# 96 token slots per expert in place of 128, operands 96 columns wide

## The chip, the cores and the metric

The kernel runs on one core of one Trainium2 chip. The metric is device time in microseconds (us). Before the change the median of three runs is 1418.41 us (1418.29 to 1418.92).

## The reference

Two decoder layers over 256 tokens of width 1024, all in fp32. Layer 0 is an mLSTM with memory attention and a dense SwiGLU. Layer 1 is multi-head latent attention with memory attention and an expert SwiGLU: the router picks 2 of 8 experts for each token. The part that matters here:

```
def moe_ffn(h, router, w_gate_up, w_down):        # D 1024, D_FF 3584, 8 experts, 256 tokens
    logits = t @ router
    top_v, top_i = lax.top_k(logits, 2)
    gates = softmax(top_v)
    for e in range(8):
        out = out + combine[:, e] * swiglu(t, w_gate_up[e], w_down[e])
```

512 assignments fall on 8 experts, 64 on the average expert. The weights of one expert are 44 MB, of all eight 352 MB.

## The kernel before, in words

Every fp32 product is made of three products of a rounded type (fp32r): each operand is cut into a high part (the value rounded) and a low part (the rest), and TensorE sums high x high, high x low and low x high in PSUM. ScalarE writes the high part of the weights (`expert_hi`, L799), VectorE the low part (`expert_lo`, L1884: ring minus high). SyncE streams weights into a ring of six slots of 1 MB (`load_expert`, L540), each slot filled by two transfers of 512 KB; it fills a slot again when its low part has been made (semaphore `lows`). High and low parts have three buffers (`CUTS`), which come free when TensorE is through with them (`through`).

The expert stage begins after the routing. Instead of all 256 tokens, an expert sees `CAP` slots: its tokens' rows are gathered into slots, 128 of them; an empty slot carries some row with gate 0, whose result goes to a spare row. If an expert has more than `CAP` tokens, all eight experts run again for the rest: `more` counts these further passes, and it is computed on the chip from the largest count. `PASSES` is 256/CAP rounded up; it bounds `more` and sets the size of the slot table in DRAM.

The order of the work is written out by hand, engine by engine; every engine walks the same loops. `expert(0)` stands alone, `Fori` runs the middle experts, and the last is again its own. An expert has seven blocks (`NBE`) of 512 hidden columns. A block is six cuts of 1 MB of weights: four for gate and up (`expert_gate_up`), two for down of the block before it (`expert_down`). A cut is 12 matmuls (`expert_cut`, L1718 to L1733): the activations are the stationary operand (128 rows of the contraction x `CAP` columns, one column for each slot), the weights are the moving operand, 512 columns wide. Then:

- ScalarE applies silu to the gate (L824, `silE`), VectorE multiplies by up (L1981, `hnE`): `CAP` partitions x 512.
- TensorE turns that with four transposes (`turn_expert`, through `tr`, L1162): source as stationary operand, identity as moving operand.
- ScalarE and VectorE cut the turned rows into high and low parts (`hidden_high` L804, `hidden_low` L1890), four chunks of `CAP` columns (`hhiE`, `hloE`).
- Next expert's rows: POOL fetches them with an indirect DMA, VectorE turns them in 32x32 squares (`turn_rows`, L1944, 16 instructions an expert, 4 in each of blocks 2 to 5), ScalarE and VectorE cut them (L759, L1960). The second expert's rows are turned by TensorE (eight transposes), the first expert's are gathered by matmuls with a matrix of zeros and ones, `Sx` (`gather`, L1689).
- An expert's result is scaled by the gate (`y_out`, L747) and added into DRAM by an indirect DMA.

The routing (`choose`, `put_slot`, L2439 to L2471) and `gates` (L1896 to L1910) are chains of small VectorE operations, each of which waits for the one before it. `gates` runs in block 2 of the first expert and computes each token's place in the slot table.

Of the kernel before, what the change touches and what calls it, by code (L numbers as in the profile page):

```python
# [18 lines left out]
ALU = mybir.AluOpType  # L19
# [4 lines left out]
I32 = mybir.dt.int32  # L24
U32 = mybir.dt.uint32

P = 128
# [1 line left out]
SLOTS = 6  # L29
SLOT = 2048  # L30
CUTS = 3
CAP = 128
NEG = -float(2.0 ** 100)
ROPE_THETA = 10000.0

# [1 line left out]
def build(nc, T, out):  # L37
    SEQ, D = T["x"].shape[1:]
    NT = SEQ // P
# [16 lines left out]
    NE = T["moe_router"].shape[2]  # L56
    HR = ROPE // 2
    assert NT == 2 and KD == 8 and NMEM == SEQ and MW == 256 and AH == 4 and BH == 6 and NOPE == P and VH == P
    PASSES = -(-SEQ // CAP)
    assert CAP <= P  # L60

    x_d, mem_d = T["x"][0], T["mem"][0]

# [91 lines left out]
    with ExitStack() as ctx:  # L155
# [5 lines left out]
        def S(name):  # L161
            if name not in sems:
                sems[name] = ctx.enter_context(nc.semaphore(name))
            return sems[name]
# [61 lines left out]
        def carve(at, *shape):  # L226
            n = int(np.prod(shape))
            v = arena[:, at:at + n]
            if len(shape) == 1:
# [36 lines left out]
        hn = carve(NT * FB, NT, FB)  # L266
        hT = carve(4096, 2, SEQ)
        silE, hnE = carve(0, EB)[0:CAP], carve(NT * FB, EB)[0:CAP]
        hhiE, hloE = (h[:, :, :].rearrange("p a s -> p (a s)")[:, 0:4 * CAP].rearrange("p (c s) -> p c s", s=CAP)
                      for h in (hhi, hlo))  # L270

        qF = carve(0, NT * BH, QKH)
# [17 lines left out]
        PT = carve(0, BH, 384)  # L290

        o = 2 * NT * FB
        Sx = carve(o, NT, CAP); o += NT * CAP
        tok_f = carve(o, NT); o += NT
        gate, gate_next = carve(o, 1)[0:CAP], carve(o + 1, 1)[0:CAP]; o += 2
        xe_ = slice(0, CAP)
        NC = PASSES * NE
        iota = carve(o, CAP); o += CAP
        iotai = arena[:, o:o + CAP].bitcast(I32); o += CAP
        m8 = carve(o, NT, 8); o += NT * 8  # L300
        idxf = carve(o, NT, 8); o += NT * 8
        idx8 = arena[:, o:o + NT * 8].bitcast(U32).rearrange("p (a b) -> p a b", a=NT); o += NT * 8
        oh1 = carve(o, NT, NE); o += NT * NE
        oh2 = carve(o, NT, NE); o += NT * NE
        picked = carve(o, NT + 1, NE); o += (NT + 1) * NE
        first_slot = carve(o, CAP); o += CAP
        key = carve(o, NT); o += NT
        ranks = carve(o, NT, NE); o += NT * NE
        hits = carve(o, 2, NT, NE); o += 2 * NT * NE
        place_at = carve(o, 3, 2 * NT); o += 6 * NT  # L310
        place_i = arena[:, o:o + 2 * NT].bitcast(I32); o += 2 * NT
        pay = carve(o, 2, NT, 3); o += 6 * NT
        raw = carve(o, 2, 3)[0:CAP]; o += 6
# [282 lines left out]
        def _(pool):  # L596
# [64 lines left out]
            for t in range(NT):  # L661
                pool.dma_start(xn[:, t], bass.AP(g1.tensor, g1.offset, [[0, P]] + [list(d) for d in g1.ap])).then_inc(S("g1_in"), 16)
            pool.wait_ge(S("att_out"), 1)
            pool.iota(iotai, pattern=[[1, CAP]], base=0, channel_multiplier=0).then_inc(S("iota"), 1)
            pool.wait_ge(S("iota"), 1)
            pool.tensor_copy(iota, iotai).then_inc(S("iota"), 1)
            pool.iota(tok_i, pattern=[[P, NT]], base=0, channel_multiplier=1).then_inc(S("iota"), 1)
# [2 lines left out]
            pool.wait_ge(S("iota"), 4)  # L670
            pool.tensor_scalar(first_slot, iota, 1.0, None, ALU.add).then_inc(S("iota"), 1)
            pool.memset(blank[:, :, 0], 0.0).then_inc(S("iota"), 1)
            pool.tensor_copy(blank[:, :, 1], iota[0:NC + 1]).then_inc(S("iota"), 1)
            pool.tensor_scalar(blank[:, :, 2], iota[0:NC + 1], float(SEQ), None, ALU.add).then_inc(S("iota"), 1)
            pool.wait_ge(S("iota"), 8)
            pool.dma_start(table_d.rearrange("(a s) c -> a s c", s=CAP), blank).then_inc(S("table_in"), 16)
            pool.dma_start(acc[SEQ:SEQ + CAP].rearrange("s (a n) -> s a n", n=P), over(ones[0:CAP, :], KD)).then_inc(S("table_in"), 16)
# [480 lines left out]
        def _(pe):  # L1158
# [527 lines left out]
            def gather(t, ks):  # L1686

                for k in ks:
                    last = mm(PS[:, 6 + k // KH, (k % KH) * CAP:(k % KH + 1) * CAP], lhsT=xn[:, t, k * P:(k + 1) * P], rhs=Sx[:, t, :],  # L1689
                              start=(t == 0 and k % KH == 0), stop=(t == NT - 1), skip_group_check=True)  # L1690
                return last

# [119 lines left out]
        def _(dve):  # L1812
# [80 lines left out]
            def gates():  # L1893

                dve.wait_ge(S("gate2_exp"), 1)
                then(v.tensor_scalar(gt2[:, 4:6], gt2[:, 2:4], 1.0, None, ALU.add))  # L1896
                then(v.reciprocal(gt2[:, 6:8], gt2[:, 4:6]))
                then(v.tensor_tensor(gt2[:, 8:10], gt2[:, 6:8], gt2[:, 2:4], ALU.mult))
                ends = [list(d) for d in ranks.ap]
                both = bass.AP(oh1.tensor, oh1.offset, ends[:1] + [[NT * NE, 2], [NE, NT], [1, NE]])  # L1900
                then(v.tensor_tensor(hits, both, bass.AP(ranks.tensor, ranks.offset, ends[:1] + [[0, 2], [NE, NT], [1, NE]]), ALU.mult))
                then(v.tensor_reduce(place_at[:, 0].rearrange("p (c t) -> p c t", c=2), hits, AX.X, ALU.add))
                then(v.tensor_scalar(place_at[:, 1], place_at[:, 0], float(CAP), float((NE - 1) * CAP), ALU.is_ge, ALU.mult))
                then(v.tensor_tensor(place_at[:, 2], place_at[:, 0], place_at[:, 1], ALU.add))
                then(v.scalar_tensor_tensor(out=place_at[:, 1].rearrange("p (c t) -> p c t", c=2), in0=bass.AP(idxf.tensor, idxf.offset, ends[:1] + [[1, 2], [NE, NT]]),
                                            scalar=float(CAP), in1=place_at[:, 2].rearrange("p (c t) -> p c t", c=2), op0=ALU.mult, op1=ALU.add))
                then(v.tensor_copy(place_i, place_at[:, 1]))
                v.tensor_copy(pay[:, :, :, 0], gt2[:, 6:10].rearrange("p (c t) -> p c t", c=2))
                for w in (1, 2):
                    last = v.tensor_copy(pay[:, :, :, w], over(tok_f, 2))  # L1910
                last.then_inc(S("gates"), 1)

            def next_dispatch(i, last):

                if isinstance(i, int):
                    dve.wait_ge(S("raw_in"), 32)
                    then(v.tensor_copy(gate, raw[:, 0, 0:1]))
                    then(v.tensor_copy(put_tok, raw[:, 0, 2:3]))
                    return
                dve.wait_ge(S("putting"), i)  # L1920
                dve.wait_ge(S("scattered"), i * 16)
                then(v.tensor_copy(gate, gate_next))
                then(v.tensor_copy(put_tok, put_next))
                if last:
                    for t in range(NT):
                        part = v.tensor_scalar(put_at[:, t:t + 1], put_next, float(t * P), None, ALU.subtract)
                    part.then_inc(S("dispatch"), 1)
                    dve.wait_ge(S("dispatch"), 3)
                    for t in range(NT):
                        part = v.tensor_scalar(Sx[:, t], iota, put_at[:, t:t + 1], None, ALU.is_equal)  # L1930
                    part.then_inc(S("dispatch"), 1)

            def next_slots(i):
# [6 lines left out]
            def turn_rows(squares):  # L1940

                for n in squares:
                    (r, c), last = divmod(n, 4), n == 15
                    done = v.transpose(xsT[32 * c:32 * c + 32].rearrange("p k (q s) -> p k q s", q=4)[:, :, r, :],  # L1944
                                       xs[32 * r:32 * r + 32].rearrange("p (k q f) -> p k q f", k=KD, q=4)[:, :, c, :])
                if last:
                    done.then_inc(S("gathered"), 1)
# [14 lines left out]
            def expert(i, last=False):  # L1962
                first = is_first(i)
                for b in range(NBE):
                    if b == 0 and not first:
                        expert_lo(i, 0, 0)
                        expert_lo(i, 0, 1)
                    if b > 0 or not first:
                        expert_lo(i, b, 2)
                        hidden_low(i * NBE + (NB + b))  # L1970
                    expert_lo(i, b, 3)
                    if b == 2 and not first and not last:
                        dve.wait_ge(S("fetching"), i)
                        next_slots(i)
                    if b > 0 or not first:
                        expert_lo(i, b, 4)
                        expert_lo(i, b, 5)
                    else:
                        expert_lo(i, 1, 0)
                    dve.wait_ge(S("silu"), i * NBE + (NB + b + 1))  # L1980
                    v.tensor_tensor(hnE, PS[0:CAP, expert_bank(i, b) + 1, :], silE, ALU.mult).then_inc(S("h_ready"), 1)  # L1981
                    if first and b == 2:
                        gates()
                    if b == (6 if first else 4 if last else 1):
                        next_dispatch(i, last)
                    if b == 5 and first:
                        next_slots(i)
                    if b < NBE - 1:
                        if b > 0 or not first:
                            expert_lo(i, b + 1, 0)  # L1990
                        expert_lo(i, b + 1, 1)
                    if 1 < b < 6 and not first and not last:
                        if b == 2:
                            dve.wait_ge(S("rows_in"), i * 16 + 16)
                        turn_rows(range(4 * (b - 2), 4 * (b - 1)))
                if not last:
                    gathered(i + 1, by_vector=not first)

# [448 lines left out]
            def put_slot(t):  # L2447

                then(v.scalar_tensor_tensor(out=key[:, t:t + 1], in0=rank_of[t][:, 0:1], scalar=1.0, in1=picked[:, t, 0:1], op0=ALU.add, op1=ALU.mult))
                return v.tensor_scalar(Sx[:, t], first_slot, key[:, t:t + 1], None, ALU.is_equal)  # L2450

            dve.wait_ge(S("iota"), 8)
            choose(0).then_inc(S("chosen"), 1)
# [66 lines left out]
```

## Time and profile before

| | |
|---|---|
| median of the runs | 1418.41 us |
| span of the profiled execution | 1417.7 us |
| TensorE matmuls busy | 1411.1 us (100%), 6721 instructions |
| weight loads busy | 1185.2 us (84%) |
| VectorE busy | 1234.8 us (87%) |
| ScalarE busy | 964.5 us (68%) |
| POOL busy | 101.9 us (7%) |
| read from HBM | 434.88 MB, 312 GB/s over the span |

Busy times of matmuls overlap: a matmul's record lasts longer than the distance to the next one's start. So a busy TensorE says little by itself, and the starts of its instructions say more. The profiled execution gives only its span; what a run's time has beyond it lies around the span.

### The profile page before, as it was taken

The numbers are of one execution on the slowest core, as the hardware profiler recorded it, in microseconds if no ns is written. First come the engines' busy times: TensorE is split into PE (matmuls) and PEld (weight loads), VectorE is DVE, ScalarE is ACT, GpSimd is POOL, SyncE is SP. The second block draws the span as 40 slices with busy tenths as digits, with TensorE's granted clock in tenths as the row PEclk, the third lists the DMA queues.
The fourth block names the chain that finished last, engine by engine and source line by source line (L and its number), as shares of the span: only waits on it lengthen the run. The fifth ranks groups of instructions, "written<-read, shape, count | busy, mean of one in ns | idle before, by whom it ended". The sixth has DMA issues, their size and how long they took to land.

```text
span 1417.7 us, 19898 instructions
## 1 busy us (share of the span) xinstructions
PE 1411.1 (100%) x6721; PEld 1185.2 (84%) x6721; DVE 1234.8 (87%) x1207; ACT 964.5 (68%) x840; POOL 101.9 (7%) x147
## 2 busy tenths in 40 slices
PE   9999999999999999999999999999999999999999
PEld 8998888888988888888888888888888888888887
DVE  6486888878677898999989999999999999999887
ACT  7465544443694677777777777787777777777775
POOL 4010000000022020010010000001001000000000
PEclk9999999999999999999999999999999999999999
DMA  9554655564445799999999999999999999999995
GB/s 321 163 180 147 219 196 178 178 204 144 127 177 194 274 384 389 375 378 393 379 382 394 374 374 396 394 374 382 393 371 382 395 382 374 395 383 382 383 393 195
DMA packets 212592, 442.93 MB, mean 312 GB/s; under 512 B 16372, under 2 KB 56760, under 8 KB 212544
## 3 DMA queue, kind: packets, MB, share of 16 engines
q1 hardware_dynamic: 208640, 430.18, 83.0%
q0 software_dynamic: 3888, 12.13, 2.9%
q8 instruction: 28, 0.46, 0.1%
q14 instruction: 20, 0.16, 0.0%
q10 hardware_dynamic: 16, 0.00, 0.0%
HBM read 434.88 MB, written 7.37 MB: 312 GB/s over the span
## 4 chain that ended last, share of the span: by engine, by line
PE 98%; ACT 1%; DVE 1%; issue 0%; POOL 0%; ACTq 0%; DVEq 0%; POOLq 0%
PE PS L1729 21%; PE PS L1730 21%; PE PS L1733 21%; PE PS L1431 5%; PE PS L1430 5%; PE PS L1432 5%; PE PS L1162 3%; PE PS L1218 2%; PE PS L1210 2%; PE PS L1212 2%; PE PS L1269 1%; PE PS L1275 1%; PE PS L1272 1%; PE PS L1718 1%; PE PS L1192 1%; PE PS L1721 1%
## 5 line engine op out<-in xcount | busy, mean ns | idle before, releaser
L1884 DVE TENSOR_TENSOR wlo<-ring,whi 128x2048 fp32r<-128x2048 f32 x334 | 758.8, 2290 | 53.3 <-ACT whi L799 51.2
L799 ACT ACTIVATE whi<-ring 128x2048 fp32r<-128x2048 f32 x334 | 639.8, 1918 | 184.3 <-PE PS L1733 173.8
L1729 PE MATMUL PS<-whi,xhi 128*128 128x512 f32 x864 | 340.8, 394 | 0.0
L1730 PE MATMUL PS<-whi,xlo 128*128 128x512 f32 x864 | 336.6, 390 | 0.0
L1733 PE MATMUL PS<-wlo,xhi 128*128 128x512 f32 x864 | 231.0, 389 | 0.0
L1733 PEld LDWEIGHTS PS<-wlo,xhi 128*128 128x128 f32 x864 | 162.1, 188 | 34.0 <-DVE wlo L1884 0.2
L1730 PEld LDWEIGHTS PS<-whi,xlo 128*128 128x128 f32 x864 | 162.4, 188 | 32.4
L1729 PEld LDWEIGHTS PS<-whi,xhi 128*128 128x128 f32 x864 | 162.3, 188 | 32.4
L1729 PE MATMUL PS<-whi,hhi 128*128 128x512 f32 x440 | 171.4, 389 | 0.0
L1730 PE MATMUL PS<-whi,hlo 128*128 128x512 f32 x440 | 171.2, 389 | 0.0
L1733 PE MATMUL PS<-wlo,hhi 128*128 128x512 f32 x440 | 117.8, 390 | 0.0
L1842 DVE TENSOR_TENSOR wlo<-ring,whi 128x2048 fp32r<-128x2048 f32 x42 | 96.0, 2289 | 11.6 <-ACT whi L766 11.2
L766 ACT ACTIVATE whi<-ring 128x2048 fp32r<-128x2048 f32 x42 | 80.5, 1916 | 26.1 <-PE PS L1432 17.7
L1733 PEld LDWEIGHTS PS<-wlo,hhi 128*128 128x128 f32 x440 | 82.6, 188 | 17.1
L1730 PEld LDWEIGHTS PS<-whi,hlo 128*128 128x128 f32 x440 | 82.6, 188 | 17.1
L1729 PEld LDWEIGHTS PS<-whi,hhi 128*128 128x128 f32 x440 | 82.6, 188 | 17.1
L1432 PE MATMUL PS<-whi,xlo 128*128 128x512 f32 x224 | 87.2, 389 | 0.0
L1430 PE MATMUL PS<-whi,xhi 128*128 128x512 f32 x224 | 87.1, 389 | 0.0
L1431 PE MATMUL PS<-wlo,xhi 128*128 128x512 f32 x224 | 87.1, 389 | 0.0
L1859 DVE STREAM_TRANSPOSE arena<-arena 32x128 f32<-32x128 f32 x208 | 63.0, 303 | 3.1
L824 ACT ACTIVATE arena<-PS 128x512 f32<-128x512 f32 x56 | 33.5, 598 | 46.2 <-PE PS L1733 46.2
L2034 DVE TENSOR_TENSOR wlo<-ring,whi 128x1536 fp32r<-128x1536 f32 (+4 forms) x27 | 48.3, 1806 | 17.8 <-ACT whi L856 17.7
(387 smaller groups left out, 1637.1 us busy)
## 6 DMA issues: line engine op xcount, KB each, us to landing
ring<-in_moe_w_gate_up SPq DMA_DIRECT2D x448, 512.0 KB, 6.7
ring<-in_moe_w_down SPq DMA_DIRECT2D x224, 512.0 KB, 7.2
ring<-in_dense_w_gate_up SPq DMA_DIRECT2D x56, 512.0 KB, 4.6
ring<-in_dense_w_down SPq DMA_DIRECT2D x28, 512.0 KB, 4.1
ring<-in_a_w_in SPq DMA_DIRECT2D x12, 768.0 KB, 8.6
ring<-in_mem_w_kv SPq DMA_DIRECT2D x4, 1024.0 KB, 7.7
ring<-in_a_w_out SPq DMA_DIRECT2D x4, 1024.0 KB, 5.3
ring<-in_b_w_out SPq DMA_DIRECT2D x4, 1024.0 KB, 7.3
```

The costliest lines, as they stand in the source:

```text
L766: nc.scalar.activation(whi[:, (FFN0 + n) % CUTS, :], ring[:, h * SLOT:(h + 1) * SLOT], ACT.Copy).then_inc(S("highs"), 1)
L799: nc.scalar.activation(whi[:, j, :], ring[:, h * SLOT:(h + 1) * SLOT], ACT.Copy).then_inc(S("highs"), 1)
L1430: mm(out_, lhsT=xh, rhs=wh, start=first, stop=False)
L1431: mm(out_, lhsT=xh, rhs=wl, start=False, stop=False)
L1432: return mm(out_, lhsT=xl, rhs=wh, start=False, stop=last)
L1729: mm(out_, lhsT=xh, rhs=whi[:, j, c0:c0 + HD], start=begin, stop=False)
L1730: mm(out_, lhsT=xl, rhs=whi[:, j, c0:c0 + HD], start=False, stop=False)
L1733: last = mm(out_, lhsT=xh, rhs=wlo[:, j, c0:c0 + HD], start=False, stop=end)
L1842: v.tensor_tensor(wlo[:, j, :], ring[:, h * SLOT:(h + 1) * SLOT], whi[:, j, :].bitcast(F32), ALU.subtract).then_inc(S("lows"), 1)
L1859: last = v.transpose(hT[cols_].rearrange("p kk (t q s) -> p t kk q s", t=NT, q=4)[:, :, :, i, :], hn[rows_].rearrange("p t (kk q f) -> p t ...
L1884: v.tensor_tensor(wlo[:, j, :], ring[:, h * SLOT:(h + 1) * SLOT], whi[:, j, :].bitcast(F32), ALU.subtract).then_inc(S("lows"), 1)
L2034: last = v.tensor_tensor(lo, src, hi.bitcast(F32), ALU.subtract)
```

## The change

`CAP` goes from 128 to 96. All views that were `CAP` wide because `CAP` was the width of a partition block are now allotted 128 and read 96 wide; the chunks of the turned silu-and-up rows lie 128 elements apart. `PASSES` becomes 3, for which the place computation gets two operations more and the routing one.

```
-CAP = 128
+CAP = 96
...
-        hhiE, hloE = (h[:, :, :].rearrange("p a s -> p (a s)")[:, 0:4 * CAP].rearrange("p (c s) -> p c s", s=CAP)
+        hhiE, hloE = (h[:, :, :].rearrange("p a s -> p (a s)").rearrange("p (c s) -> p c s", s=P)[:, :, 0:CAP]
...
-                    last = mm(PS[:, 6 + k // KH, (k % KH) * CAP:(k % KH + 1) * CAP], lhsT=xn[:, t, k * P:(k + 1) * P], rhs=Sx[:, t, :],
+                    last = mm(PS[:, 6 + k // KH, (k % KH) * CAP:(k % KH + 1) * CAP], lhsT=xn[:, t, k * P:(k + 1) * P], rhs=Sx[:, t, 0:CAP],
...
                 then(v.tensor_tensor(place_at[:, 2], place_at[:, 0], place_at[:, 1], ALU.add))
+                for q in range(2, PASSES):
+                    then(v.tensor_scalar(over_at, place_at[:, 0], float(q * CAP), float((NE - 1) * CAP), ALU.is_ge, ALU.mult))
+                    then(v.tensor_tensor(place_at[:, 2], place_at[:, 2], over_at, ALU.add))
...
-                    (r, c), last = divmod(n, 4), n == 15
-                    done = v.transpose(xsT[32 * c:32 * c + 32].rearrange("p k (q s) -> p k q s", q=4)[:, :, r, :],
+                    (r, c), last = divmod(n, 4), n == CAP // 8 - 1
+                    done = v.transpose(xsT[32 * c:32 * c + 32].rearrange("p k (q s) -> p k q s", s=32)[:, :, r, :],
...
-                        turn_rows(range(4 * (b - 2), 4 * (b - 1)))
+                        turn_rows(range(CAP // 32 * (b - 2), CAP // 32 * (b - 1)))
```

The loop `for q in range(2, PASSES)` behind the largest count, which is in the kernel already (L2468), ran no times with two passes and runs once with three. The slot table's fill on POOL (L672 to L674) goes over 25 x 96 entries for 17 x 128.

## Rows read from the trace of the kernel before

**Rows 1.** Page, part 4: the chain that ended last, by engine.
```profile
PE 98%; ACT 1%; DVE 1%; issue 0%; POOL 0%; ACTq 0%; DVEq 0%; POOLq 0%
```

**Rows 2.** Chain of waits, 900 to 936 us: start us, us, what, how many links.
```profile
901.40 0.44 PE PS L1162 x4
...
903.69 0.91 PE PS L1733 x4
...
906.41 0.91 PE PS L1733 x4
...
918.20 0.44 PE PS L1162 x4
```

**Rows 3.** Stretch, us; busy us of PE, PEld, DVE, ACT, POOL; clock, DMA share, GB/s.
```profile
1054.00:1171.00 117.00, 117.00 (x531) 96.91 (x530) 111.10 (x79) 88.60 (x59) 5.57 (x4) 1.00 1.04 384
```

**Rows 4.** Waits of SyncE's queue: us in total, times, longest us.
```profile
SPq L540 <- DVE wlo L1884: 555.7, 328, 17.5
```

**Rows 5.** Chain of waits ahead of the expert stage: 4-column stationary, 384, 320 wide.
```profile
26.15 0.44 PE PS L1162 x4
...
29.39 1.39 PE PS L1218 x8
...
369.29 1.17 PE PS L1218 x8
```

**Rows 6.** Groups by form, whole span: matmuls (PE) and weight loads (PEld).
```profile
L1162 PE MATMUL PS<-ident,arena 128*128 128x128 f32 x298 | 43.6, 272 | 0.0
L1192 PE MATMUL PS<-memv,xT 128*128 128x64 f32 x64 | 7.5, 276 | 0.1
L1689 PE MATMUL PS<-arena,xn 128*128 128x128 f32 x32 | 4.0, 278 | 0.0
L1162 PE MATMUL PS<-ident,arena 73*128 73x73 f32 x1 | 0.2, 227 | 0.0
...
L1733 PEld LDWEIGHTS PS<-wlo,xhi 128*128 128x128 f32 x864 | 162.1, 188 | 34.0 <-DVE wlo L1884 0.2
L1162 PEld LDWEIGHTS PS<-ident,arena 128*128 128x128 f32 x298 | 36.3, 140 | 8.2 <-issue 0.3
L1162 PEld LDWEIGHTS PS<-ident,arena 128*96 128x96 f32 x16 | 1.8, 126 | 0.1
L1162 PEld LDWEIGHTS PS<-ident,arena 128*4 128x4 f32 x4 | 0.3, 84 | 0.1
```

**Rows 7.** Timeline around the 73-wide transpose: start us, us, engine, line.
```profile
15.61 0.23 PE L1162 MATMUL PS<-ident,arena 73*128 73x73 f32 x1
...
15.67 0.38 PE L1162 MATMUL PS<-ident,xT 128*128 128x128 f32 x2
```

**Rows 8.** VectorE's groups by form, 1054 to 1171 us.
```profile
L1884 DVE TENSOR_TENSOR wlo<-ring,whi 128x2048 fp32r<-128x2048 f32 x43 | 97.6, 2289 | 5.0 <-ACT whi L799 4.7
L1944 DVE STREAM_TRANSPOSE xT<-xn 32x256 f32<-32x256 f32 x16 | 7.0, 436 | 0.3
...
L1890 DVE TENSOR_TENSOR hlo<-PS,hhi 128x512 fp32r<-128x512 f32 x7 | 4.8, 684 | 0.0
L1960 DVE TENSOR_TENSOR xlo<-xT,xhi 128x1024 fp32r<-128x1024 f32 x1 | 1.2, 1214 | 0.0
```

**Rows 9.** Chain of waits by line, 505 to 525 us, around `gates`.
```profile
by line: PE PS L1733 34.0%; PE PS L1729 32.9%; PE PS L1730 32.9%; PE PS L1162 2.2%
```

**Rows 10.** Timeline: end of the routing, and `gates`.
```profile
467.88 2.28 DVE L1884 TENSOR_TENSOR wlo<-ring,whi 128x2048 fp32r<-128x2048 f32 x1
...
472.29 0.39 PE L1729 MATMUL PS<-whi,xhi 128*128 128x512 f32 x1
...
508.14 2.29 DVE L1884 TENSOR_TENSOR wlo<-ring,whi 128x2048 fp32r<-128x2048 f32 x1 [0.43 <-ACT whi L799]
...
512.00 0.17 DVE L1903 TENSOR_SCALAR arena<-arena 128x4 f32<-128x4 f32 x1
```

**Rows 11.** Timeline of POOL: the fill of the slot table.
```profile
439.91 2.62 POOL L674 TENSOR_SCALAR arena<-arena 17x128 f32<-17x128 f32 x1
```

More of the change, by code:

```diff
@@ L59, in build @@
     PASSES = -(-SEQ // CAP)
-    assert CAP <= P
+    assert CAP <= P and CAP % 32 == 0
     x_d, mem_d = T["x"][0], T["mem"][0]
@@ L292, in build @@
         o = 2 * NT * FB
-        Sx = carve(o, NT, CAP); o += NT * CAP
+        Sx = carve(o, NT, P); o += NT * P
         tok_f = carve(o, NT); o += NT
@@ L297, in build @@
         NC = PASSES * NE
-        iota = carve(o, CAP); o += CAP
-        iotai = arena[:, o:o + CAP].bitcast(I32); o += CAP
+        iota = carve(o, P); o += P
+        iotai = arena[:, o:o + P].bitcast(I32); o += P
         m8 = carve(o, NT, 8); o += NT * 8
@@ L305, in build @@
         picked = carve(o, NT + 1, NE); o += (NT + 1) * NE
-        first_slot = carve(o, CAP); o += CAP
+        first_slot = carve(o, P); o += P
         key = carve(o, NT); o += NT
@@ L310, in build @@
         place_at = carve(o, 3, 2 * NT); o += 6 * NT
+        over_at = carve(o, 2 * NT); o += 2 * NT
         place_i = arena[:, o:o + 2 * NT].bitcast(I32); o += 2 * NT
@@ L663, in _ @@
             pool.wait_ge(S("att_out"), 1)
-            pool.iota(iotai, pattern=[[1, CAP]], base=0, channel_multiplier=0).then_inc(S("iota"), 1)
+            pool.iota(iotai, pattern=[[1, P]], base=0, channel_multiplier=0).then_inc(S("iota"), 1)
             pool.wait_ge(S("iota"), 1)
@@ L672, in _ @@
             pool.memset(blank[:, :, 0], 0.0).then_inc(S("iota"), 1)
-            pool.tensor_copy(blank[:, :, 1], iota[0:NC + 1]).then_inc(S("iota"), 1)
-            pool.tensor_scalar(blank[:, :, 2], iota[0:NC + 1], float(SEQ), None, ALU.add).then_inc(S("iota"), 1)
+            pool.tensor_copy(blank[:, :, 1], iota[0:NC + 1, 0:CAP]).then_inc(S("iota"), 1)
+            pool.tensor_scalar(blank[:, :, 2], iota[0:NC + 1, 0:CAP], float(SEQ), None, ALU.add).then_inc(S("iota"), 1)
             pool.wait_ge(S("iota"), 8)
@@ L1929, in next_dispatch @@
                     for t in range(NT):
-                        part = v.tensor_scalar(Sx[:, t], iota, put_at[:, t:t + 1], None, ALU.is_equal)
+                        part = v.tensor_scalar(Sx[0:CAP, t], iota[0:CAP], put_at[:, t:t + 1], None, ALU.is_equal)
                     part.then_inc(S("dispatch"), 1)
@@ L2449, in put_slot @@
                 then(v.scalar_tensor_tensor(out=key[:, t:t + 1], in0=rank_of[t][:, 0:1], scalar=1.0, in1=picked[:, t, 0:1], op0=ALU.add, op1=ALU.mult))
-                return v.tensor_scalar(Sx[:, t], first_slot, key[:, t:t + 1], None, ALU.is_equal)
+                return v.tensor_scalar(Sx[:, t, 0:CAP], first_slot[:, 0:CAP], key[:, t:t + 1], None, ALU.is_equal)
             dve.wait_ge(S("iota"), 8)
```

## The prediction

> **What bounds the kernel now.** I read the chain of waits first, because every engine but one could be hidden. The chain gives TensorE 98% of the span [rows 1]: the reader should look for any other engine in it and find 2% in all. So only what shortens or stalls TensorE's stream can move the time. Next I read that chain inside the expert stage. Cuts follow each other every 2.72 us (the low parts at 903.69 and 906.41), and a cut is 12 matmuls: 0.2267 us from start to start, which I call the pitch. The four transposes of a block take 0.44 us, a pitch of 0.109, and blocks of six cuts follow every 16.79 us (transposes at 901.40 and 918.20) [rows 2]. That is 72 x 0.2267 + 4 x 0.109 = 16.76, so a block holds nothing but its matmuls and transposes. An expert is 7 blocks, 117.5 us; eight of them are 940 us, two thirds of the time. The granted clock is 1.00 there, the 2.4 GHz level, while VectorE is busy 111.1 of 117 us and ScalarE 88.6 [rows 3]: VectorE is 5% from being the bound. SyncE, which issues the weight transfers, waits 555.7 us for VectorE to free ring slots [rows 4], so the DMA is ahead of need and not the bound, though its share stands at 1.04 [rows 3].
>
> **What the change does not touch.** The weights are the moving operand, 512 wide, and all of them still pass: 8 x 42 x 12 = 4032 expert matmuls of 512 columns before and after. The change narrows the stationary operand from 128 to 96 columns. What sets the pitch? Eight links of 384 columns take 1.39 us (0.1737 each) and eight of 320 take 1.17 (0.1463) [rows 5], against 0.2267 for 512. The slope is (226.7 - 173.7)/128 = 0.41 ns a column, one column per cycle at 2.4 GHz, and about 13 ns are left over at each width (226.7 - 213.3). The weight load of these matmuls lasts 188 ns and 34.0 us of idle over 864 loads, 39 ns each, lie before it [rows 6]; since it lies beside the matmul before it, and since 320 columns go at 146 ns with the same load, the load is not what is waited for. Narrower loads are therefore worth 0 in my sum. The bound on that: the 13.3 ns left over may belong to the load. No row has a narrow load of the rounded type. Four transposes whose stationary operand has only 4 columns run at 0.44 us [rows 5], the same 0.109 as with 128 columns, although their loads are shorter (84 ns at 4 columns, 126 at 96, 140 at 128) [rows 6]. That is the nearest row, and it says 0. If the rest went in proportion to width, 13.3/4 x 4032 = 13.4 us would go; if it vanished, 53.6.
>
> The Trainium skill bears on this in "TensorE: Matmul & The Clock Gate", section "Back-to-back issue gap": in a stream of load and matmul pairs the spacing is set by both. Its section "LDWEIGHTS" makes the load proportional to columns, P/1.2 ns, so 27 ns less at 96 columns; if all of it showed in the pitch the time would fall by an estimated 108 us, to 1304. The trace does not agree for widths of 320 to 512, where the spacing follows the moving width alone [rows 5].
>
> **Transposes.** Each block turns its hidden rows with four transposes (tr in turn_expert). Source rows are the stationary operand (now 96 partitions x 128 columns), and the moving operand is the identity, now 96 x 96 for 128 x 128. So here the moving width does fall. The group of 128-wide ones has 272 ns each, the single 73-wide one 227 [rows 6]: 45 ns for 55 columns, 0.82 ns a column, two cycles. And the transpose behind the 73-wide one starts 0.06 us after it [rows 7] where 128-wide ones are 0.109 apart: (109 - 62)/55 is the same slope. At 96 columns: 32 x 0.82 = 26 ns less each. There are 8 x 7 x 4 = 224 in blocks: 5.9 us, all on the path. The eight transposes that turn the second expert's rows (turn_rows on TensorE) give 8 x 26 ns = 0.2. Bounds: 0 if a floor of the pitch holds at 109 for another reason (the 96 source partitions, or the pieces around a transpose), 9 us if the two seams of each block (the links into and out of its transposes) shrank by 26 ns each as well, 2 x 56 x 26 ns = 2.9 more. I take the 5.9, the value of the row that has a narrow transpose.
>
> **The gather** (L1689) multiplies by Sx, 128 wide before and 96 now, in full fp32. Its matmuls last 278 ns; L1192's, only 64 wide, 276 [rows 6]. So width below 128 buys nothing there: 0, at most 32 x 26 ns = 0.8.
>
> **VectorE and ScalarE.** In an expert L1944 falls from 16 to 12 squares (4 x 436 ns), L1890 goes from 512 to 384 elements and L1960 from 1024 to 768. From 684 and 1214 ns for 512 and 1024 elements [rows 8] an element costs 1.035 ns, so these save 7 x 132 and 265 ns. Together 1.7 + 0.9 + 0.3 = 2.9 us of 111 an expert; ScalarE's copies of the same tiles shrink likewise. TensorE hides all of it, so the value is 0, and it only widens the cover of the 5%. The chunks now lie 128 apart with 96 used; L1960 already reads and writes rows 256 apart with 128 used, and its 1214 ns are less than twice the 684 of the packed L1890 with half the elements, so I put nothing on the stride. L1981 and y_out keep their free size, and partitions are not what their time hangs on.
>
> **What is added.** Three passes in place of two, since 256/96 rounds up to 3. On VectorE: two small operations in gates and one in the routing, at 0.17 us each, by such an operation in gates [rows 10], with 0.03 to the next. Behind those in gates stand the low parts L1884 of the next block, 0.4 us later, in the first expert alone. The chain nowhere names VectorE in that stretch [rows 9], and the L1884 ahead of gates had 0.43 us of idle before it, so VectorE has room to catch up [rows 10]; TensorE waits for nobody else's work in it. The one in the routing stands ahead of L1884 at 467.88, whose result is wanted after 472 [rows 10]; it delays nothing. If the cover were gone the three would cost 0.6 us. POOL fills 25 x 96 table rows for 17 x 128: its longest fill of 2.62 us ends at 442.5 [rows 11], 20 us before anything asks for the table, so 0. Fewer gathered rows (96 x 4 KB) relieve the DMA by under 1% of an expert's 44 MB.
>
> **The sum.** 5.9 + 0.2 = 6.1 us. The span of the profiled execution is 1417.7, 0.7 below the median 1418.41 of the runs; I take the 0.7 as lying around the span and unchanged. 1417.7 - 6.1 = 1411.6, plus 0.7 is 1412.3.
>
> **The rivals.**
> R1, the transposes give nothing: their pitch stays at 0.109 because something other than the moving width sets it. For it: 4-column loads change nothing, so a floor is conceivable, and only one narrow transpose stands in a running stream. Against: that one went faster. The time: 1418.4.
> R2, the pitch follows the stationary width too: 13.4 us more in proportion, 1399. At the most the pitch is 213.3 ns, an expert 42 x 12 x 0.2133 + 28 x 0.083 = 109.8 us, and VectorE is then the bound, 108.2 busy and the 5.0 of idle that it has before L1884 [rows 8], 113.2: 8 x (117.5 - 0.8 - 113.2) = 28, 1384. Against: the 4-column transposes.
> R3, the slower side: a load of 96 columns is a slower kind of load and comes to stand between matmuls. The place is the load before each of the 4032 matmuls. It decides once the record of 188 ns grows past the pitch, 227. From the rows a load of this type costs 84 + 0.81 x columns, so 162 at 96; if the column part doubled, 240, and the pitch rose by 13.6 ns: 54.8 us, 1412.3 + 54.8 = 1467. Against: plain fp32 loads at 128, 96 and 4 columns lie on one line (140, 126, 84) [rows 6], with no step where 96 leaves the full width.
> Also against: the load of the rounded type, 188 ns, is longer than the plain fp32 one of 140, so it does not look like a fast kind that could be lost.
> A rule of the Trainium skill would bring R3 about ("TensorE: Matmul & The Clock Gate", section "Weight-path perf modes — Fast Weight Load (FWL) and DoubleRow"): fast load is on only with 128 weights and a type that isn't fp32. If the rounded type counts as other than fp32, the change turns it off, with R3's time; if it counts as fp32, nothing changes.
> R4, the change doesn't hold what it promises: an expert with more than 96 tokens adds a pass of all eight experts, 940 us, 2352. The reference run on its inputs routes 55, 50, 53, 70, 61, 75, 78 and 70 tokens, so the highest has 18 to spare; what is left is the inputs being others.
>
> **How the numbers follow.** About 0.2%, 2.8 us, is what a measurement of this kernel tells from no change. Forecast 0.68; R1 0.12; R2 0.12, most of it at its proportional end; R3 with any lesser rise of the pitch 0.07; R4 0.01. Faster by over 0.2%: the forecast and R2, 0.80. Within 0.2%: R1, 0.12. Slower: R3 and R4, 0.08. The range goes from 1398 (R2 in proportion, with the gather's 0.8) to 1420 (R1 with the additions uncovered, and the scatter of runs); it leaves out R2's far end, R3 and R4. The forecast alone spans 1408 to 1413.5.
>
> **What would show it.** Transposes in the expert stage at 0.083 us from start to start in the chain, 0.33 for four; blocks at 16.68 apart for 16.79; matmuls of 512 at 0.2267 as before, though their load falls to about 162 ns; VectorE busy 108 of 117 us. The forecast is wrong if the 512-wide pitch differs by even 1 ns (4 us), or if transposes keep 0.109, or if a wait appears in a block that has none now.

## The result: slower, and the profile after

Before: 1418.92 us (median of 5 runs, 1418.29 to 1423.6). After: 1424.82 us (median of 5, 1424.67 to 1425.19). The ratio is 1.0038, 95% interval 1.0026 to 1.0051. The forecast was 1412.3 with a range to 1420, so the time lies outside it and on the other side of no change. The profiled execution of after took 1424.82 us with a span of 1423.0, 5.3 longer than before's.

The page's busy times (part 1) and the chain by engine (part 4) still say that TensorE is everything:

```profile
PE 1416.3 (100%) x6721; PEld 1073.9 (75%) x6721; DVE 1218.2 (86%) x1186; ACT 956.6 (67%) x840; POOL 99.3 (7%) x147
...
PE 98%; ACT 1%; DVE 1%; issue 0%; POOL 0%; ACTq 0%; DVEq 0%; POOLq 0%
```

So the bound did not move; its own stream became longer. The chain of waits of after, 900 to 936 us (start us, us, what, links; L1163 and L1734 are L1162 and L1733 of before):

```profile
903.48 0.33 PE PS L1163 x4
905.65 0.92 PE PS L1734 x4
...
908.41 0.92 PE PS L1734 x4
...
920.37 0.33 PE PS L1163 x4
```

Beside [rows 2] two things changed. Four transposes take 0.33 us where they took 0.44, as forecast. Cuts follow every 2.76 us (905.65 and 908.41) where it was 2.72, so a 512-wide matmul starts every 0.230 us and no longer every 0.2267, and the blocks are 16.89 us apart and no longer 16.79. I then took the mean of the start-to-start times of 512-wide expert matmuls between 700 and 1290 us, without the one long step behind each block's transposes: 227.0 ns before, 230.0 after. In the steady part of a block they come at 226, 227, 227 before; after, the sequence 229, 231, 232, 228 repeats. It is a small loss everywhere and no stall anywhere.

The stretch of one expert, in the columns of [rows 3], has the same granted clock, 1.00, so the clock did not do it:

```profile
1054.00:1171.00 117.00, 117.00 (x528) 82.56 (x527) 108.11 (x74) 86.89 (x58) 5.54 (x4) 1.00 1.03 379
```

The groups by form, whole span (busy us, mean ns | idle before), answer to [rows 6]:

```profile
L1163 PE MATMUL PS<-ident,arena 96*128 96x96 f32 x224 | 27.7, 246 | 0.0
L1690 PE MATMUL PS<-arena,xn 128*128 128x96 f32 x32 | 3.9, 276 | 0.0
...
L1734 PEld LDWEIGHTS PS<-wlo,xhi 128*96 128x96 f32 x864 | 139.2, 161 | 59.6 <-DVE wlo L1885 0.3
L1163 PEld LDWEIGHTS PS<-ident,arena 96*128 96x128 f32 x224 | 25.0, 140 | 9.0
```

The weight load of the 512-wide matmuls fell from 188 to 161 ns, and the idle time before the loads of this group grew from 34.0 to 59.6 us. The load is shorter and has more slack, and yet the matmul beside it starts later.

VectorE's groups in 1054 to 1171 us (as in [rows 8]) and POOL's fill (start us, us; as in [rows 11]):

```profile
L1885 DVE TENSOR_TENSOR wlo<-ring,whi 128x2048 fp32r<-128x2048 f32 x42 | 95.8, 2290 | 8.9 <-ACT whi L800 8.4
L1948 DVE STREAM_TRANSPOSE xT<-xn 32x256 f32<-32x256 f32 x12 | 5.2, 435 | 0.2
...
L1891 DVE TENSOR_TENSOR hlo<-PS,hhi 128x384 fp32r<-128x384 f32 x7 | 3.9, 550 | 0.0
L1964 DVE TENSOR_TENSOR xlo<-xT,xhi 128x768 fp32r<-128x768 f32 x1 | 0.9, 944 | 0.0
```

```profile
439.32 2.54 POOL L675 TENSOR_SCALAR arena<-arena 25x96 f32<-25x96 f32 x1
```

**Where the time went.** In a block, 71 steps from one 512-wide matmul to the next are 3.0 ns longer each, +0.21 us; three steps between its transposes are 26 ns shorter each, -0.08; and the seam, the step from the first to the second 512-wide matmul behind the transposes, is 0.03 shorter (below). Together +0.10, and the measured blocks are 16.79 and 16.90 (mean over many). 56 blocks make +6.2. The work ahead of the expert stage was 0.5 us shorter in this execution, and all of it lies before 55 us, ahead of the first line that changed: it is no effect of the change. The rest, -0.4, was not followed further.

The seam is in the timeline of after behind the transposes (start us, us, engine, line):

```profile
903.31 0.49 PE L1163 MATMUL PS<-ident,arena 96*128 96x96 f32 x4
903.59 0.45 PE L1730 MATMUL PS<-whi,xhi 128*96 128x512 f32 x1
903.88 0.39 PE L1731 MATMUL PS<-whi,xlo 128*96 128x512 f32 x1
904.11 0.39 PE L1730 MATMUL PS<-whi,xhi 128*96 128x512 f32 x1
```

The second 512-wide matmul comes 0.29 us after the first, where the next ones come after 0.23. It is the one long step of a block. The runs w128 and b96 below show on what its length depends.

### The profile page after: what moved, and what is told of

Same layout as the page of the kernel before. It is cut to its first block, busy times and chain, and to the rows that moved or that the text cites. A ratio compares the mean times of both kernels' runs of the same rounds, so it can differ in the third digit from the quotient of the medians.

```text
span 1423.0 us, 19877 instructions
## 1 busy us (share of the span) xinstructions
PE 1416.3 (100%) x6721; PEld 1073.9 (75%) x6721; DVE 1218.2 (86%) x1186; ACT 956.6 (67%) x840; POOL 99.3 (7%) x147
## 4 chain that ended last, share of the span: by engine, by line
PE 98%; ACT 1%; DVE 1%; issue 0%; POOL 0%; ACTq 0%; DVEq 0%; POOLq 0%
PE PS L1734 21%; PE PS L1730 21%; PE PS L1731 21%; PE PS L1433 5%; PE PS L1431 5%; PE PS L1432 5%; PE PS L1163 3%; PE PS L1219 2%; PE PS L1211 2%; PE PS L1213 2%; PE PS L1270 1%; PE PS L1276 1%; PE PS L1273 1%; PE PS L1719 1%; PE PS L1193 1%; PE PS L1722 1%
## 5 line engine op out<-in xcount | busy, mean ns | idle before, releaser
L1730 PE MATMUL PS<-whi,xhi 128*96 128x512 f32 x864 | 341.1, 395 | 0.0
L1731 PE MATMUL PS<-whi,xlo 128*96 128x512 f32 x864 | 338.3, 392 | 0.0
L1734 PE MATMUL PS<-wlo,xhi 128*96 128x512 f32 x864 | 233.8, 392 | 0.0
L1734 PEld LDWEIGHTS PS<-wlo,xhi 128*96 128x96 f32 x864 | 139.2, 161 | 59.6 <-DVE wlo L1885 0.3
L1731 PEld LDWEIGHTS PS<-whi,xlo 128*96 128x96 f32 x864 | 139.5, 161 | 56.2
L1730 PEld LDWEIGHTS PS<-whi,xhi 128*96 128x96 f32 x864 | 139.4, 161 | 56.1
L1730 PE MATMUL PS<-whi,hhi 128*96 128x512 f32 x440 | 172.4, 392 | 0.0
L1731 PE MATMUL PS<-whi,hlo 128*96 128x512 f32 x440 | 172.3, 392 | 0.0
L1734 PE MATMUL PS<-wlo,hhi 128*96 128x512 f32 x440 | 119.3, 392 | 0.0
L1843 DVE TENSOR_TENSOR wlo<-ring,whi 128x2048 fp32r<-128x2048 f32 x42 | 96.0, 2289 | 11.5 <-ACT whi L767 11.0
L1734 PEld LDWEIGHTS PS<-wlo,hhi 128*96 128x96 f32 x440 | 71.0, 161 | 30.2
L1433 PE MATMUL PS<-whi,xlo 128*128 128x512 f32 (+1 forms) x224 | 87.2, 389 | 0.0
```

The source lines that it names most:

```text
L1433: return mm(out_, lhsT=xl, rhs=wh, start=False, stop=last)
L1730: mm(out_, lhsT=xh, rhs=whi[:, j, c0:c0 + HD], start=begin, stop=False)
L1731: mm(out_, lhsT=xl, rhs=whi[:, j, c0:c0 + HD], start=False, stop=False)
L1734: last = mm(out_, lhsT=xh, rhs=wlo[:, j, c0:c0 + HD], start=False, stop=end)
L1843: v.tensor_tensor(wlo[:, j, :], ring[:, h * SLOT:(h + 1) * SLOT], whi[:, j, :].bitcast(F32), ALU.subtract).then_inc(S("lows"), 1)
```

## The experiments

Fifteen kernels beside the two. Runs of one batch are compared with the kernel before on the same chip: 1419.06 us (w128, w112, w64, w32), 1419.23 (b96, ar0, ar24, n256), 1418.73 (sh32, sh16, ar248, w64e), 1419.37 (pad32, sh8, sh24). Where no interval is given the kernel ran once. "Pitch" is the mean start-to-start of the 512-wide expert matmuls, 700 to 1290 us, without the seam. "Block" is the mean distance between the first transposes of neighbouring blocks, in the same stretch.

My theory at the start: the narrower stationary operand itself makes each 512-wide matmul start later. The rivals: something else of the change does it (the layout of the chunks 128 apart, the other timing of VectorE and the DMA), or the loss goes by a law in the number of columns.

**w128: everything of the change, but the expert matmuls read 128 stationary columns again**

```
+MW_ = 128
+hhiM, hloM = (... p (c s) -> p c s, s=P)[:, :, 0:MW_] ...
+xm_ = slice(0, MW_)
-(PS[0:CAP, ...], xhi[..., xe_], xlo[..., xe_], ...      # and the same for hhiE, hloE
+(PS[0:MW_, ...], xhi[..., xm_], xlo[..., xm_], ...
```

> The changed kernel, but the expert matmuls read and write all 128 stationary columns again (columns 96 to 127 hold old values whose output rows nobody reads); everything else stays at 96 slots. Width theory (the 3.3 ns more per matmul come from the narrower stationary operand): the distance from start to start of 512-wide matmuls returns to 226.7 ns, a block takes 16.68 us, the time is 1412 to 1413 us, below both kernels. Layout theory (they come from something else in the change, such as the 96-partition transposes or the rows 128 apart): it stays at 230 ns, 16.90 us a block, 1425 us.

Measured: 1414.85 us (6 runs, 1414.2 to 1414.98), ratio to before 0.9969 [0.9957, 0.9981]; span 1413.2. Its chain of waits, 900 to 936 us:

```profile
909.61 0.91 PE PS L1738 x4
...
912.33 0.91 PE PS L1738 x4
...
915.95 0.33 PE PS L1167 x4
```

Cuts are 2.72 us apart again (pitch 227.0 ns) and the transposes keep their 0.33. The 96 slots, the chunks 128 apart, the three passes and the short transposes are all still there, so none of them makes the matmuls later: the loss comes with the width of the expert matmuls' stationary operand. It is also the fastest kernel of the study. Its block is 16.713 us, 0.077 less than before's, which is three steps of 26 ns and not four. The timeline of the seam shows where the fourth is.

```profile
915.79 0.49 PE L1167 MATMUL PS<-ident,arena 96*128 96x96 f32 x4
916.07 0.48 PE L1734 MATMUL PS<-whi,xhi 128*128 128x512 f32 x1
916.38 0.39 PE L1735 MATMUL PS<-whi,xlo 128*128 128x512 f32 x1
```

From the first to the second 512-wide matmul it is 0.31 us here and 0.29 in after. The means over 700 to 1290 us are 314 ns before, 314 in w128 and 287 in after. So with short transposes and 188 ns loads the seam keeps its length, and the fourth 26 ns are not gained; with short transposes and 161 ns loads they are. With the runs that follow, all with short transposes, the seam is 314, 299, 287, 285 and 284 ns at loads of 188, 174, 161, 134 and 109 ns: it shrinks with the load down to 161 ns and hardly further.

**w112, w64, w32: the same with 112, 64 and 32 columns** (`MW_ = 112`, `64`, `32`; w64 and w32 leave out the results of the slots beyond their width)

> As w128, with 112 stationary columns. Width theory in proportion to the missing columns: 228.3 ns from start to start, about 1419 us. Width theory as a step (any width under 128 costs the same): 230 ns, 1425 us. Layout theory: 230 ns, 1425 us; it is told apart by w128.

> As w128, with 64 stationary columns; the outputs of slots 64 to 95 are left out. In proportion to the missing columns: 233.3 ns, about 1439 us. As a step: 230 ns, 1425 us. If only widths that are no power of two suffer: 226.7 ns, 1412 us.

> As w64, with 32 stationary columns; the outputs of slots 32 to 95 are left out. In proportion: 236.7 ns, about 1453 us. As a step: 230 ns, 1425 us. Power of two: 226.7 ns, 1412 us.

| stationary columns | 128 | 112 | 96 (after) | 64 | 32 |
|---|---|---|---|---|---|
| time, us | 1414.85 | 1421.42 | 1424.82 | 1424.53 | 1429.62 |
| pitch, ns | 227.0 | 228.8 | 230.0 | 229.9 | 231.5 |
| its load, ns | 188 | 174 | 161 | 134 | 109 |

Weight loads by form, 700 to 1290 us, of w64 and then of w32:

```profile
L1738 PEld LDWEIGHTS PS<-wlo,xhi 128*64 128x64 f32 x540 | 72.2, 134 | 51.4
```

```profile
L1735 PEld LDWEIGHTS PS<-whi,xlo 128*32 128x32 f32 x540 | 59.3, 110 | 63.6
```

The load lies near a straight line, 84 + 0.81 x columns, as the prediction had it. The pitch does not follow the load: the shortest load has the latest matmuls. So it is not the length of the load that holds the matmuls back. Nor is the loss proportional to the missing columns: 96 and 64 are equal, and from 128 to 112 more than half of the 3.0 ns is already there.

**b96: the kernel before, with 96 columns in the expert matmuls and nothing else** (the edit of w128, on before, with `MW_ = 96`)

> The kernel before (128 slots) in which only the expert matmuls take 96 stationary columns (slots 96 to 127 are left out; no expert has so many tokens). If the width alone makes the cost and the change's other edits do not matter: 230 ns from start to start, transposes stay at 108.5 ns. A block gains 72 x 3.3 = 0.24 us, less the shorter link behind the transposes (0.03): 16.79 + 0.21 = 17.00 us, in all 12 us, 1431 us. If the cost needs the change's other edits, 1419 us.

Measured: 1430.73 us (4 runs, 1430.32 to 1431.07), ratio 1.0079 [1.0063, 1.0096]. Chain of waits, 900 to 936 us:

```profile
900.08 0.92 PE PS L1737 x4
...
902.84 0.92 PE PS L1737 x4
...
906.52 0.44 PE PS L1166 x4
...
923.53 0.44 PE PS L1166 x4
```

Cuts 2.76 apart, transposes 0.44, blocks 17.01: +11.5 us for the width alone. The block follows from the parts: 16.79 + 0.21 (the pitch) = 17.00, measured 17.005. With w128 this closes the account from both sides: the width costs 10.0 us (after against w128) to 11.5 (b96 against before), and the rest of the change gives 4.2 back (w128 against before).

The seam did not shrink, though I had expected 0.03 of it (start us, us, engine, line):

```profile
906.72 0.48 PE L1733 MATMUL PS<-whi,xhi 128*96 128x512 f32 x1
907.03 0.39 PE L1734 MATMUL PS<-whi,xlo 128*96 128x512 f32 x1
```

It is 0.31 us (316 ns in the mean) with a 161 ns load behind 128-wide transposes. So a narrow load alone does not shorten the seam, and short transposes alone do not either (w128): it takes both. By which mechanism stays open.

**n256: after, with each 512-wide matmul as two of 256**

```
+def mm2(out_, lhsT, xw, j, c0, start, stop):
+    mm(out_[:, 0:256], lhsT=lhsT, rhs=xw[:, j, c0:c0 + 256], ...)
+    return mm(out_[:, 256:512], lhsT=lhsT, rhs=xw[:, j, c0 + 256:c0 + 512], ...)
```

> The changed kernel (96 columns) with each 512-wide expert matmul as two of 256. At 128 stationary columns 256-wide ones run at 120.0 ns in another stage. If the excess is a fixed amount for each matmul and load: 123.3 ns, 8064 of them, about 1490 us. If it goes with the moved columns: 121.7 ns, about 1477 us. If it is a matter of the load's timing beside the matmul, neither number need hold.

Measured: 1466.43 us. This asked whether the 3 ns come once for each matmul or with each moving column. The answer is neither: the 256-wide matmuls start every 116.1 ns (116.0 on the hidden rows), while the expectations were 123.3 and 121.7. The kernel before has 256-wide ones with 128 stationary columns at 120.0, sixteen in 1.92 us of its chain:

```profile
387.75 1.92 PE PS L1218 x16
```

So at 256 moving columns no loss from the narrow operand is seen, and the spacing is 4 ns shorter. That is not a clean measurement of the width: the matmuls of before stand in another stage and change their stationary operand each time, those of n256 take the same one twice in a row.

Blocks inside an expert are 17.05 us apart; the excess over the 16.90 of after is the pitch (2 x 116.1 = 232.1 for 230.0). Most of the time lost lies elsewhere, once in each of five middle experts, behind the transposes of its first block. The chain of waits, 820 to 840 us, and the group with most idle, 700 to 1290 us:

```profile
828.26 1.92 ACT whi L800
830.18 2.50 issue
832.68 0.52 PE PS L1711
833.21 0.21 PE PS L1712
```

```profile
L1711 PE MATMUL PS<-whi,xhi 128*96 128x256 f32 x524 | 150.5, 287 | 20.3 <-issue 20.3
```

TensorE stood idle there for about 4 us, 20.3 us in five such places, and no releaser is shown for it. Behind the pause its matmuls come every 0.21 us for a while, at the lower clock level of 1.2 GHz: the granted clock is 0.57 over 829.8 to 836.5 us, and 0.97 over 700 to 1290. A block with such a pause takes 23 to 24 us, 6 to 7 us more than the others. The cause of the pause was not looked for.

**ar0, ar24, ar248: the kernel before, 128 columns, with the gathered rows xhi and xlo at another address**

```
+padA = [P, 4096] (ar0), [P, 4120] (ar24), [P, 4344] (ar248)    # floats ahead of xA, over the arena
+xA = [P, 2, KD, SEQ];  xhiA, xloA = xA[:, 0], xA[:, 1]
-xhi[..., xe_], xlo[..., xe_]       # in the copies, the low parts and the gate-and-up matmuls
+xhiA[..., xe_], xloA[..., xe_]
```

In before, xhi, hhi, whi and wlo all begin at an address that leaves 128 when divided by 1024 (bytes in a partition). ar0 puts the gathered rows at 160, ar24 at 256, ar248 at 128 again, far from the old place. In the expectations, the address or phase theory is that the pitch depends on where the stationary operand lies; phase means its place relative to the moving one.

> The kernel before with the experts' gathered rows (xhi and xlo in the expert stage alone) moved to an address 32 bytes off a 64-byte line, as the memory-attention projections have theirs, whose matmuls at 128 stationary columns run at 233.3 ns. Address theory: the distance depends on how the stationary operand's reads fall on the memory's lines, so the gate-up matmuls (2688 of 4032) go to 233 ns and the down matmuls stay at 226.7: +17 us, 1436 us. Theory of width alone: 226.7 for all, 1419 us, and the projections are slow for another reason.

> As ar0, moved 96 bytes further to an address that is a multiple of 128 bytes. Address theory: 226.7 ns again, 1419 us. If instead being far from the weights' buffers or in the upper part of the memory were the cause: as ar0.

> As ar0 (128 slots, gathered rows moved up in the memory), but at an address that leaves the same rest modulo 1024 bytes as xhi and as the weights' buffers (128). Phase theory: 226.7 ns everywhere, 1419 us. If the region of the memory is the cause: 233 ns in the gate-up matmuls, 1434 us, as ar0 and ar24.

| | ar0 | ar24 | ar248 | before |
|---|---|---|---|---|
| time, us | 1434.66 | 1434.27 | 1419.29 | 1419.23 |
| pitch of matmuls on the gathered rows, ns | 233.1 | 232.7 | 227.2 | 227.2 |
| block, us | 17.077 | 17.07 | 16.79 | 16.79 |

The chain of ar0, 900 to 936 us:

```profile
904.43 0.91 PE PS L1737 x4
907.15 0.91 PE PS L1737 x4
908.06 0.44 PE PS L1166 x4
910.36 0.93 PE PS L1737 x4
913.16 0.93 PE PS L1737 x4
915.96 0.93 PE PS L1737 x4
```

Two kinds of cut stand side by side in one kernel. Ahead of the transposes are the cuts on the hidden rows, which were not moved: 2.72 apart. Behind them are the cuts on the moved rows: 2.80 apart. Both have full width and 188 ns loads. The groups by form of ar0, 700 to 1290 us, say the same in their means, 395 against 389:

```profile
L1734 PE MATMUL PS<-whi,xA 128*128 128x512 f32 x533 | 210.5, 395 | 0.0
...
L1734 PE MATMUL PS<-whi,hlo 128*128 128x512 f32 x276 | 107.4, 389 | 0.0
```

And of ar248, where only the address differs from ar0:

```profile
L1734 PE MATMUL PS<-whi,xA 128*128 128x512 f32 x540 | 210.4, 390 | 0.0
```

So the pitch depends on where the stationary operand lies, at an unchanged width, load and count. An address costs up to 6 ns, twice what the change cost. That the remainders by 1024 are what counts is more than these runs show: the hidden rows' four chunks lie 512 bytes apart, so every other one leaves 640 and not 128, and their matmuls still start every 226.7 ns in before.

The Trainium skill says in "TensorE: Matmul & The Clock Gate", section "Step-by-step: what each phase is for", that TensorE reads its two operands through separate ports and that loading the next weights takes no read bandwidth from the running matmul. As a statement about time that does not fit ar0 against ar248: with the same 188 ns load, which has slack in both, the matmuls start 6 ns later or not according to the address that is loaded from. The measurement decides. That the two reads get in each other's way is the near explanation, and no run here shows it.

**pad32: the kernel before, with everything 32 bytes higher** (`+sb("pad0", [P, 8])` ahead of the ring)

> The kernel before with every buffer moved up by 32 bytes: stationary and moving operands together, so that their places relative to each other stay as they were. If what counts is the stationary operand's place relative to the moving one: 226.7 ns in the expert and dense stages, 1419 us. If it is each operand's own place on the memory's lines: 233 ns as in ar0, in the dense and expert stages alike, 1445 us or more.

Measured: 1419.29 us, pitch 227.0, blocks 16.79. Chain, 900 to 936 us:

```profile
903.56 0.91 PE PS L1734 x4
906.28 0.91 PE PS L1734 x4
```

Here every buffer has moved, the stationary and the moving operands together, by the 32 bytes that the gathered rows alone were off in ar0, and nothing changes. So what counts is not the stationary operand's own address but its place relative to something that moved with it. The moving operand is the likely one; the weights' ring and the other buffers moved too, and no run separates them.

**sh32, sh16, sh8, sh24, w64e: after, its 96 columns moved inside the chunk of 128** (w64e: w64 with the columns 64 to 127, most results left out)

```
-hhiE, hloE = (...)[:, :, 0:CAP]
+hhiE, hloE = (...)[:, :, 32:32 + CAP]         # sh16: 16, sh8: 8, sh24: 24
-xe_ = slice(0, CAP)
+xe_ = slice(32, 32 + CAP)
```

My theory by then was one of phase: what counts is where the last stationary column lies. Columns 32 to 127 end where 128 columns end, so by it sh32 was to be as fast as 128 columns: 226.7 ns and 1411 us.

> The changed kernel with its 96 stationary columns kept in columns 32 to 127 of each 128-column chunk in place of 0 to 95, for xhi, xlo, hhi and hlo, written and read alike. [...] Theory of width alone: 230 ns and 1425 us.

> As sh32 with columns 16 to 111. Phase theory: neither end lies as in the kernel before; like w112, whose last column is the same one, 228.8 ns, about 1420 us. Width alone: 230 ns, 1425 us.

> As sh16 with columns 8 to 103 (32 bytes up). If the distance goes smoothly over the address, between 230.0 (0 bytes) and 228.3 ns (64 bytes): 229 ns, 1421 us. If it jumps with every 32 bytes, as 128 columns do from 226.7 to 233.3: 231 ns or more, above 1425 us.

> As sh16 with columns 24 to 119 (96 bytes up). Smooth between 228.3 (64 bytes) and 231.7 ns (128 bytes): 230 ns, 1425 us. With jumps: other than that.

> As w64 (64 stationary columns, most output left out), but columns 64 to 127 of each chunk in place of 0 to 63, so that the last column lies as in the kernel before. Phase theory: 226.7 ns, about 1411 us. Width alone: 229.9 ns as w64, 1424 us.

| | after | sh8 | sh16 | sh24 | sh32 |
|---|---|---|---|---|---|
| shift, bytes | 0 | 32 | 64 | 96 | 128 |
| time, us | 1424.82 | 1420.6 | 1418.55 | 1427.01 | 1431.56 |
| pitch, ns | 230.0 | 229.1 | 228.4 | 230.7 | 231.7 |
| block, us | 16.90 | 16.833 | 16.78 | 16.94 | 17.018 |

sh32 ran 4 times (1431.05 to 1431.77), ratio to before 1.009 [1.0073, 1.0107]. w64e: 1423.88 us, pitch 229.9, the same as w64. The chains of sh32 and of sh16, 900 to 936 us:

```profile
911.53 0.93 PE PS L1734 x4
...
914.31 0.93 PE PS L1734 x4
```

```profile
905.73 0.91 PE PS L1734 x4
...
908.47 0.91 PE PS L1734 x4
...
917.60 0.33 PE PS L1163 x4
```

Cuts are 2.78 apart in the one and 2.74 in the other, at one width, with loads of 161 to 162 ns and short transposes in all. sh32 was to be the best of them and is the worst, so that theory fell. What is left is the fact: the loss depends on the place, it is least at 64 bytes of the five shifts tried, and with 64 columns a shift of 256 bytes (w64e) changes nothing. sh16 and sh8 each ran once; sh16, at 1418.55 us, is level with before (1418.73).

**What stays open.** Why the width and the place of the stationary operand move the pitch, and by which rule. The moving operand alone was not moved. A narrower stationary operand also makes the output narrower, 96 partitions of PSUM for 128, and no run separates the two. Whether some layout with 96 columns is as fast as 128 is not known; the best seen is 228.4 ns. Shown is only this: 96 columns in place of 128 at the old place cost 3.0 ns a matmul, another place at a fixed width up to 6, and 227.0 was reached only with 128 columns and the operands laid out to each other as in before.

## Why the prediction was wrong

- **What bounds the kernel: right.** TensorE is 98% of the chain after as before, at the same clock, and VectorE stayed hidden.
- **"What the change does not touch": the step that failed.** It put the narrower loads at 0 for 4032 matmuls. The matmuls with narrow stationary operands cost 3.0 ns more each, 12.1 us (w128 and b96 show that it is the width). By the prediction's own sign of being wrong, a pitch off by 1 ns, it was off by three. The section bounded the step from the gain side alone (13.4 and 53.6 us); the one loss that was priced, R3, needed a load longer than the pitch. The evidence for 0 was the transposes with a stationary operand of 4 columns. They are another kind (plain fp32, 128 moving columns, 0.109 us of pitch), and they do not tell of a few ns on a 512-wide stream. In n256, at 256 moving columns, no loss is seen either: what one form of matmul does says little about another. Why the width costs these 3.0 ns stays open.
- **Transposes: right in the pitch, with luck in the count.** 0.33 for four, 83 ns each. The prediction took four steps of 26 ns in a block. The transposes give three; the fourth comes only where the load of the 512-wide matmuls is narrow as well (after, against w128 and b96), which the prediction did not have. In w128 the span is 1413.2, against 1411.6 by the sum: 56 x 26 ns = 1.5 is this fourth step.
- **Gather: right.** 276 ns for 278, and nothing gained. **VectorE: right.** 550 and 944 ns for the forecast 552 and 949, 108.1 us an expert for the forecast 108. **What is added: right.** POOL's fill is 2.54 us for 2.62, and w128 carries all additions and is faster than before by what its transposes give.
- **The 0.7 around the span** was a mistake of mine: it is the span of one execution taken from the median of others. Where time and span belong to the same execution they are 1.8 apart in after (1424.82 less 1423.0) and 1.7 in w128. It is 1 us at most and changes nothing in the account.
- **R3** had the right side and place and the wrong mechanism. It needed the load's record to grow past the pitch of 227; the record fell to 161, just as forecast, and the loss came all the same. Its line for the load, 84 + 0.81 x columns, came out, but with luck: the prediction had one row of this type, at 128 columns, and its 84 is the figure of a plain fp32 load. Its chance of 0.07 covered "any lesser rise of the pitch", which is what happened, and was too small. R1, R2 and R4 fell: the transposes gave their part, the pitch rose and did not fall, and no pass was added (6721 matmuls before and after).
- The sum with the measured terms, the 12.1 of the pitch, the 6.1 of the transposes and the 0.5 ahead of the stage: 1417.7 + 12.1 - 6.1 - 0.5 = 1423.2, for a measured span of 1423.0.

There was a clue in the trace of before, and I did not use it. The memory projections have the same width, type and 188 ns loads as the expert matmuls, but a stationary operand at another place (it leaves 160 when divided by 1024). Chain of waits of before, around 58 us and around 140 us:

```profile
58.59 1.87 PE PS L1218 x8
...
140.61 1.81 PE PS L1454 x8
```

That is 0.234 us a matmul in the one and 0.226 in the other (a dense stage, whose rows lie at 128). Two pitches for one form of matmul in one trace mean that something beside width sets it, and a change that touches the stationary operand 4032 times should have had that unknown in its range: as an estimate, 4032 x 7 ns = 28 us on the slower side.

## What to carry to other kernels

When one engine is the whole chain, a change to the form of its repeated instruction has no neutral price: bound it from both sides, and multiply 1 ns by the count first (4 us here). A smaller operand need not be a cheaper one. The gain of this change is had by narrowing only where the moving width shrinks (the transposes) and leaving the 512-wide matmuls at 128 stationary columns: 1414.85 us, ratio 0.9969. And look whether one form of instruction shows two durations in the trace before: the difference names a variable that the sum doesn't have.

## What the runs showed of the hardware that I had not expected

- 512-wide matmuls of the rounded type start every 227.0 ns with 128 stationary columns (226.7 in the steady part of a block), and every 228.8, 230.0, 229.9 and 231.5 ns with 112, 96, 64 and 32, although their loads shrink from 188 to 109 ns.
- At 128 columns the same matmul starts every 233 ns when the gathered rows, its stationary operand, are moved to an address whose remainder by 1024 is 32 or 128 bytes off (ar0, ar24). It starts every 227 ns when they are moved far away with the remainder kept (ar248), and also when all buffers move by 32 bytes (pad32).
- At 256 moving columns, matmuls with 96 stationary ones start every 116.1 ns in n256, and with 128 every 120.0 in another stage of before: the loss seen at 512 does not show.
- Behind four transposes the second 512-wide matmul starts 314 to 316 ns after the first in before, in w128 (short transposes, 188 ns load) and in b96 (long transposes, 161 ns load), and 287 ns after it in after, which has both short. Three of the four shortened steps were gained without the narrow load, and all four with it.
